# A two-layer decoder step: the indexer-key pages fetched by SyncE, one plain DMA a page, in place of GpSimd's indirect DMAs

## What is computed

```
ki_past = cki[page_table].reshape(B, past, IDX_DIM)
ki_all  = jnp.concatenate([ki_past, ki_new], axis=1)
sc      = indexer_scores(qi, wi, ki_all, q_pos, jnp.arange(L))
_, sel  = lax.top_k(sc, topk)
```

## Time and profile before

| | |
|---|---|
| median of 3 runs | 1708.08 us |
| lowest, highest | 1706.55, 1710.25 us |
| profiled execution, span | 1881.7 us; the page gives no other time of it |
| granted TensorE clock, mean | 0.859 of full speed |
| TensorE busy | 1567.8 us (83%) |
| VectorE, ScalarE, GpSimd busy | 850.0, 482.0, 272.5 us |
| GpSimd page gathers (L626) | 128, 122.0 us busy |
| DMA | 116.45 MB, mean 62 GB/s |

### The profile page before, as it was taken

One profiled execution on the slowest core, in us unless ns is written; L12 is line 12 of the kernel. 1 busy time (PEld: TensorE's weight loads), 2 busy tenths in 40 slices (PEclk: granted clock), 3 DMA queues, 4 the chain that ended last, 5 costly groups with the idle time before them and its releaser, 6 DMA issues.

```text
span 1881.7 us, 29237 instructions
## 1 busy us (share of the span) xinstructions
PE 1567.8 (83%) x10216; PEld 1330.8 (71%) x10216; DVE 850.0 (45%) x1731; ACT 482.0 (26%) x867; POOL 272.5 (14%) x260
## 2 busy tenths in 40 slices
PE   5369967748979999999862999766698999999996
PEld 3146644426969999999830758543487999998996
DVE  1003875624375555642210268753334655557221
ACT  4011301313342222332120132023234322224221
POOL 3710020150020000000176002004102000000002
PEclk8579977657989999999965996957678999999997
DMA  5112101010223333323311211011002233332331
GB/s 163 53 59 59 24 6 53 6 41 1 68 57 90 90 93 95 92 77 93 97 46 44 82 24 23 6 54 32 15 23 68 68 90 92 94 92 73 93 96 46
DMA packets 189622, 116.45 MB, mean 62 GB/s; under 512 B 25716, under 2 KB 184908, under 8 KB 189306
## 3 DMA queue, kind: packets, MB, share of 16 engines
q1 hardware_dynamic: 183246, 102.50, 19.7%
q0 software_dynamic: 6272, 12.63, 2.4%
HBM read 111.30 MB, written 4.44 MB: 62 GB/s over the span
## 4 chain that ended last, share of the span: by engine, by line
PE 72%; issue 12%; DVE 7%; ACT 3%; another core or an unknown queue 2%; DMA 1%; POOL 1%; DVEq 1%; SPq 0%; ACTq 0%; POOLq 0%
PE ps L740 44%; PE ps L725 6%; PE ps L765 4%; PE ps L837 3%; PE ps L984 2%; PE ps L1005 2%; PE ps L828 2%; PE ps L993 1%; POOL xT L620 1%; PE ps L854 1%; PE ps L712 1%; PE ps L788 1%; PE ps L1031 1%; DVE TS L1451 1%
## 5 line engine op out<-in xcount | busy, mean ns | idle before, releaser
L740 PE MATMUL ps<-moR_r,W_r 128*128 128x260 f32 x1408 | 284.8, 284 | 0.0
L740 PEld LDWEIGHTS ps<-moR_r,W_r 128*128 128x128 f32 x1408 | 219.0, 190 | 0.0
L620 POOL TENSOR_TENSOR xT<-xT,moR 128x520 f32<-128x520 f32 x32 | 45.6, 1462 | 1031.9 <-DVE moR L1468 1031.9
L740 PE MATMUL ps<-hT_r,QZC_r 128*128 128x260 f32 x896 | 183.9, 287 | 0.0
L725 PE MATMUL ps<-hT,W 128*128 128x260 f32 x576 | 163.4, 431 | 0.0
L765 PE MATMUL ps<-W,hT 128*128 128x328 f32 (+1 forms) x160 | 81.2, 609 | 94.5 <-issue 91.6
L740 PE MATMUL ps<-moR_r,QZC_r 128*128 128x260 f32 x704 | 148.5, 293 | 12.1 <-DVE hT_r L1810 11.8
L740 PE MATMUL ps<-moR_r,SQ_r 128*128 128x260 f32 x704 | 143.7, 285 | 0.0
L740 PEld LDWEIGHTS ps<-hT_r,QZC_r 128*128 128x128 f32 x896 | 142.4, 194 | 0.0
L740 PE MATMUL ps<-hT_r,SQ_r 128*128 128x260 f32 x704 | 141.4, 282 | 0.0
L765 PEld LDWEIGHTS ps<-W,hT 128*128 128x128 f32 (+1 forms) x160 | 33.4, 223 | 139.3 <-issue 129.4
(11 more groups left out here) (328 smaller groups left out, 3063.0 us busy)
## 6 DMA issues: line engine op xcount, KB each, us to landing
W<-in_w_gate SPq DMA_DIRECT2D x44, 512.0 KB, 3.9
W<-in_w_val SPq DMA_DIRECT2D x44, 512.0 KB, 3.9
W<-in_w_down SPq DMA_DIRECT2D x16, 1408.0 KB, 7.0
W<-in_w_in SPq DMA_DIRECT2D x8, 1024.0 KB, 5.6
W<-in_w_in SPq DMA_DIRECT2D x16, 256.0 KB, 4.2
W<-in_w_out SPq DMA_DIRECT2D x16, 256.0 KB, 4.1
W<-in_w_out SPq DMA_DIRECT2D x8, 512.0 KB, 5.1
yR<-in_x_prompt SPq DMA_DIRECT2D x1, 2048.0 KB
```

What stands on the lines that cost most here:

```text
L620: nc.gpsimd.tensor_tensor(xT[:, k, :], xT[:, k, :], mo[:, k, :], ALU.add).then_inc(x_ready.sem, 1)
L740: last = mm(ps[:, 2 * (g % 2) + f, 0:HT], w(k), x(k)[:, f * HT:(f + 1) * HT], start=(k == 0 and n == 0), stop=(k == nk - 1 and n == 2))
```

## The change

SyncE now fetches the pages. For each of the 128 pages of a layer it loads the page number from the table `PT` in SBUF into a register (`value_load`), computes the address, and issues one DMA of 64 rows of 512 bytes into 64 partitions; even pages go to the lower 64 partitions, odd ones to the upper. The first 64 pages stand behind `load(1)`, the other 64 behind `load(2)`. SyncE waits for the page table at the start of the program (`const_in`), and for `x_turned` ahead of the pages. `idxI`, its constant `row64` and the step on it are gone; GpSimd issues no DMA for pages. The words on constants that only go away are left out of the diff:

```diff
--- before
+++ after
...
@@ -288,7 +287,6 @@
         att = sb("att", [P, 4, 4])
 
         PT = sb("PT", [P, NB, NPG], I32)
-        idxI = sb("idxI", [P, NB, NPP], I32)
         phys = sb("phys", [P, 2, NB, NPP])
         base = sb("base", [P, 1])
         qib = sb("qib", [P, NB, 16])
...
@@ -323,7 +321,7 @@
         w_in_slot = [Signal("w_in_slot0", 16 * SLOT_DMAS[0]), Signal("w_in_slot1", 16 * SLOT_DMAS[1])]
         w_val_slot = [Signal(f"w_val_slot{u}", 16 * NF // 2) for u in range(2)]
         vec_in = Signal("vec_in", 16 * 9)
-        pages_in = Signal("pages_in", 16 * 64)
+        pages_in = Signal("pages_in", 16 * NB * NPG)
         prep_mm = Signal("prep_mm", 1)
         prep_ev = Signal("prep_ev", 4)
         x_ready = Signal("x_ready", 16)
...
@@ -466,6 +463,7 @@
                          A["page_table"].rearrange("b j -> (b j)").partition_broadcast(P)).then_inc(const_in.sem, 16)
             sp.dma_start(x_rows, A["x_prompt"][0].rearrange("(t p) d -> p t d", p=P)).then_inc(x_in.sem, 16)
             sp.dma_start(xs_rows, A["x_sample"][:, 0, :]).then_inc(x_in.sem, 16)
+            sp.wait_ge(const_in.sem, 32)
 
             def layer(l):
                 w_in = A["w_in"][l].rearrange("(k p) n -> p k n", p=P)
...
@@ -502,6 +500,17 @@
                                      ).then_inc(s, 16)
 
 
+                def index_pages(batches):
+                    cache = A["cache_idx_k"][l]
+                    sp.wait_ge(x_turned.sem, KD)
+                    for b in batches:
+                        for j in range(NPG):
+                            page = sp.value_load(PT[0:1, b, j:j + 1], min_val=0, max_val=N_PHYS - 1)
+                            pp, g = divmod(j, 2)
+                            sp.dma_start(IK[64 * g:64 * g + 64, NPP * b + pp, :],
+                                         cache[bass.ds(page, 1)].rearrange("n (r e) d -> (n r) (e d)", e=2)
+                                         ).then_inc(pages_in.sem, 16)
+
                 wait_alone(sp, *so_ev(l, 0))
                 v = vec_rows
                 for a, name in enumerate(("g_pre_mix", "g_post_mix", "g_pre_ffn", "g_post_ffn")):
...
@@ -518,8 +527,10 @@
                 wait_alone(sp, *tile_done(l, 0))
                 load(0)
                 load(1)
+                index_pages(range(0, NB // 2))
                 wait_alone(sp, *kv_mm(l, 5))
                 load(2)
+                index_pages(range(NB // 2, NB))
                 for c in (3, 4):
                     wait_alone(sp, *tile_done(l, 2 * (c - 2)))
                     load(c)
...
@@ -601,10 +612,9 @@
 
         @block.gpsimd
         def _(gp):
-            page_pairs = A["cache_idx_k"].rearrange("l n (r e) d -> (l n r) (e d)", e=2)
             k_rows = A["cache_k"].rearrange("l n r h d -> (l n r) (h d)")
             v_rows = A["cache_v"].rearrange("l n r h d -> (l n r) (h d)")
-            gp.wait_ge(tables.sem, 3)
+            gp.wait_ge(tables.sem, 1)
             gp.wait_ge(x_turned.sem, KD)
 
             def cos_part(l, j):
...
@@ -621,14 +631,6 @@
                                             ).then_inc(x_ready.sem, 1)
 
             def layer(l):
-                wait_alone(gp, *tile_done(l, 0))
-                for j in range(64):
-                    nc.gpsimd.indirect_dma_start(
-                        IK[:, j, :], None, page_pairs,
-                        bass.IndirectOffsetOnAxis(ap=idxI[:, j // NPP, j % NPP:j % NPP + 1], axis=0)
-                    ).then_inc(pages_in.sem, 16)
-
-
                 wait_alone(gp, *rstd_ready(l, 1))
                 for j in range(4):
                     wait_alone(gp, *evac(l, XP_T + j + 1))
...
@@ -654,10 +656,6 @@
                 for j in range(4, 8):
                     cos_part(l, j)
 
-                wait_alone(gp, *pages_in(l, 16 * 64))
-                nc.gpsimd.tensor_scalar(idxI[:, :, :], idxI[:, :, :], float(N_PHYS * 64), None, ALU.add
-                                        ).then_inc(pool_step.sem, 1)
-
                 wait_alone(gp, *list_ready(l, 1))
                 gp.dma_start(scratch.rearrange("b (h i) -> h b i", h=16), ixi[:, :, :]).then_inc(list_out.sem, 16)
                 wait_alone(gp, *list_out(l, 16))
...
@@ -670,7 +668,6 @@
                                 dst[:, 2 * b + t, :], None, rows,
                                 bass.IndirectOffsetOnAxis(ap=IDX[:, b, t:t + 1], axis=0)).then_inc(s.sem, 16)
                 add_updates(l, 0)
-                wait_alone(gp, *pool_step(l, 1))
                 add_updates(l, KD)
 
             with gp.Fori(0, DEPTH) as l:
...
@@ -855,7 +852,7 @@
                                   KIS[:, g % 2, i * P:(i + 1) * P], qib[:, q // NPP, :], start=True, stop=True)
                     last.then_inc(sdot_mm.sem, 1)
 
-                pe.wait_ge(*pages_in(l, 16 * 64))
+                pe.wait_ge(*pages_in(l, 16 * NB * NPG))
                 for g in range(16):
                     pe.wait_ge(*(dot_relu(l, 24) if g < 2 else pg_ev(l, g - 1)))
                     for i in range(4):
```

More of the change, by code:

```diff
@@ L53 @@
           ("swap", P), ("mask", 896), ("same", 64), ("below", 64), ("newneg", 1), ("newrow", 64),
-          ("newto", 64), ("diag", 8), ("iota16", 16), ("tok", 1), ("row64", 1), ("edge", 60), ("wsel", 32),
+          ("newto", 64), ("diag", 8), ("iota16", 16), ("tok", 1), ("edge", 60), ("wsel", 32),
           ("bits", 32)]
@@ L106, in constants @@
     put("tok", np.arange(P)[:, None])
-    put("row64", np.arange(P)[:, None] % 64)
     put("edge", np.array([[w / min(t + 1, w) for t in range(POOL_BUF)] for w in WINDOWS]).reshape(1, 60))
@@ L428, in build @@
         ffn_step = Steps("ffn_step", 5)
-        pool_step = Signal("pool_step", 1)
         SQUARES_ROOM = (4, 4, KD, 2)
@@ L1435, in _ @@
             dve.wait_ge(const_in.sem, 32)
[L1436 to L1439, removed]
             nc.vector.tensor_copy(phys[:, :, :, :], PT[:, :, :].rearrange("p b (j two) -> p two b j", two=2)
```

## The result

| | median, us | runs from to, us |
|---|---|---|
| before, on the same chip | 1709.16 | 1706.55 to 1718.23 |
| after | 1910.7 | 1902.9 to 1912.31 |

After / before is 1.1152, 95% interval 1.1113 to 1.119: slower by 201.5 us. The forecast was slower, 1876 us between 1760 and 2015: the sign and the mechanism came, the size was 35 us short. The profiled execution of the changed kernel took 1911.08 us, its span is 1909.2 us: this time the profile and the timed runs agree, where before they were 174 us apart.

The account below looks back on a forecast made before the run. TensorE's order of work was taken to count, its stalls beside gathers mostly the profile's. Weights queued behind SyncE's page steps came late: 80.2 + 81.0 + 7 for restarts = 168 us on 1708, 1876 us, range 1760 to 2015.

Parts of the forecast that it names:

- the two places named: TensorE waits some 17 us for chunk 2 after two indexer-query tiles, some 60 us for chunk 3 before the first pooling tile.
- Removed gathers: On GpSimd, 128 gathers of 0.951 us leave; nobody waits for them in time, so worth 0.
- the stalls: TensorE's stalls beside gathers, together 160 us, belong mostly to the profiled execution; the 105 us beside page gathers cannot be won.
- B: Rival: the stalls beside the gathers are real in timed runs too, and go; 63 us slower, 1771 us; chance 0.08.
- C: Rival: the stalls are real and the page step is below 1.0 us; 1656 us at 0.80; chance 0.05.
- A: Rival: the register load is about free (0.04), step 0.7 us; 14 us a layer, about 1740 us; chance 0.05.
- D: Rival: the step costs more than 1.8 us, up to 2.45; 307 us more, 2183 us; chance 0.06.
- The step: On SyncE, one page's issue: 0.48 ordinary issue, 0.17 extra register instructions, 0.60 register load; 1.25 us.
- The restarts: TensorE starts at a low granted clock after idling: 2 us a restart, 7 us in all.
- part 2: SyncE's price for the pages: 1.25 us a step, 80 us for 64 steps, 160 us for 128.
- Part 3: Weight chunks queue behind SyncE's page steps: chunk 3 late for the first pooling tile by 80.2 and 81.0 us.
- The stalls at the key and value gathers: In TensorE's profile, excess of 23.8 us in layer 0, 31.0 in layer 1; to stay, span about 1944 us.

Follow-up runs that it names:

- run 3: The changed kernel without the range check on each page number (two check instructions a step): 1834.62 us, ratio 1.073 to the kernel before.
- 4: The changed kernel with the same 128 DMAs but constant page numbers, so no register load and no check: 1739.27 us, ratio 1.017 to the kernel before.
- run 7: The changed kernel with one register load for four page numbers and no check, steps placed as in the change: 1781.67 us, ratio 1.0405 to the kernel before.
- 8: The changed kernel with grouped register loads, no check, steps divided 44, 32 and 52 behind chunks 1, 2 and 4: 1701.7 us, ratio 0.9949 to the kernel before.
- run 2: The kernel before without its page gathers, GpSimd filling the page buffer with a constant instead: 1713.08 us, ratio 1.0029.
- run 10: The kernel before plus one line of the change, SyncE waiting for the page table before its first small loads: 1707.48 us, ratio 1.0005.
- run 1: The kernel before, unedited, measured and profiled anew: 1710.38 us, ratio 1.002, profiled span 1697.4 us.
- 9: The changed kernel with grouped loads, no check and divided steps, measured a second time beside the kernel before: 1700.56 us, ratio 0.9952.
- run 11: The changed kernel with a layer's 128 page steps replaced by two plain 2 MB DMAs behind chunk 1: 1704.32 us, ratio 0.9964 to the kernel before.

## Why the prediction was right, and where it was short

**Right: what decides.** The chunks stand behind 64 and 128 steps, and TensorE waits for them at the two places named, ended by a DMA into `W`; runs 3, 4 and 7 scale as the step does, and 8 takes the delay away by place and price together. Removed gathers are worth 0 (run 2), the wait for the page table 0 (run 10).

**Right: the stalls.** They were not to be won (runs 1 and 2), so B and C fall on their common condition. C needed a step below 1.0 us as well; run 7 has one, 0.85 us, and is slower by 72.5 us. The prediction's A and D fall by the step, 1.34 us.

**The step: 1.34 us measured, 1.25 predicted, by errors that cancel.** SyncE's groups on the lines of a page step in the changed kernel, as min/median/max ns:

```profile
L508 SPq TENSOR_LOAD <-PT x256: 262/268/484, 24.4 to 1124.1; - x128
L508 SPq FUSED_REGOPS  x256: 161/164/179, 24.9 to 1124.4; - x128
L508 SPq SEQ_ASSERT  x256: 18/18/37, 25.1 to 1124.6; - x128
...
L510 SPq FUSED_REGOPS  x256: 113/113/127, 25.2 to 1124.7; - x128
L510 SPq MOVE yR<-in_cache_idx_k x256: 29/29/38, 25.4 to 1124.9; - x128
L510 SPq DMA_DIRECT2D yR<-in_cache_idx_k x256: 468/469/600, 25.5 to 1124.9; - x128
```

The register load, put at 0.60, is 0.268 us (0.33 less): the geometric middle of the two bounds, 0.27, which the prediction worked out and passed over, was the better choice; 0.60 was the middle of two guesses and rests on no row. The DMA was taken from a row of another shape at 0.296 and is 0.469 (0.17 more). Three register instructions at 0.037 became four of 0.164, 0.018, 0.113 and 0.029, together 0.324 for 0.111 (0.21 more): one that checks a range or computes an address from a register is not the one that a fixed address has. The gaps are 0.28 (0.04 more). In all 0.09 us over. That 1.25 came so near is luck: with 0.27 for the load and the rest as it stood, the step would have been 0.92 and the forecast 1876 - 256 x 0.33 = 1792 us.

On the load, the Trainium skill's "DMA: Bandwidth & Descriptors", section "Latency and other measured facts", has a floor of about 600 ns for a `tensor_load`. The row above and that of run 3 have medians of 268 and 267 ns over 256 loads each, so here the measurement decides:

```profile
L508 SPq TENSOR_LOAD <-PT x256: 260/267/488, 24.8 to 1049.4; - x128
```

**The 35 us.** TensorE waited 33.23 + 65.66 = 98.9 us in layer 0 and 96.2 in layer 1, where the prediction had a lateness of 80.2 and 81.0: 34 us more. The restarts, put at 7 us in all, took 2.8 + 2.3 us in layer 0 and 2.5 + 2.2 in layer 1 (tiles of 9.98, 9.48, 9.68 and 9.34 us for 7.18): 9.8. Of layer 0's 18.7 us, 15.8 lie in the first wait: it was to be 109.6 - 92.2 = 17.4 us and was 33.2. Two sources of about equal size are behind the error in layer 0:

- Chunk 3 was to be there at 190.1 and its tile began at 202.58, 12.5 us later: 128 x 0.09 = 11, and the steps began at 24.4 and not at 24.0. That is the step of part 2.
- The tile was wanted earlier. Part 3 had it "for the first pooling tile at 157.58 - 47.7 = 109.9"; without any stall (run 1) it is at 97.27, 12.6 us sooner. The stall was taken out at 0.398 us a record, the pace of the 16 records before it; undisturbed, 48 of them take 13.60 us, 0.283 each, so 40 x (0.398 - 0.283) = 4.6 us were left in. The other 8.0 lie ahead of the stretch: its last 40 records (41, counted by TensorE's own) began at 57.5 in the first profile and at about 60.8 - 40 x 0.283 = 49.5 in run 1. Only the part from 57.5 on had been looked at as disturbed.

These are 25 us, and the waits of layer 0 are only 18.7 over. In the changed kernel's execution TensorE was 2.3 us later at the 48 records than in run 1 (49.62 for 47.28), and the first restart's 2.8 us stand in another term; 1 us is left. In layer 1 the waits are 15 us over; 11 of them are the step again.

**Wrong: what the profile would show.** The stalls at the key and value gathers were to stay, with a span near 1944. From 418 to 461 us, the stretch where they would be in layer 0 (GpSimd issues its 32 gathers there), TensorE is busy 35.29 of 43 us:

```profile
418.00:461.00 43.00, 35.29 (x167) 21.05 (x166) 22.65 (x51) 19.02 (x47) 30.75 (x32) 0.84 0.19 50
```

The span is 1909.2, 2 us from its own time. None of the later profiled executions shows them. The prediction took them for the profiler's, and they were that one execution's. What slowed that one execution stays open; it did not come back.

**Open: the last 0.5%.** Runs 8, 9 and 11 are 0.36 to 0.51% faster than before, run 2 is not (1.0029). The gathers on GpSimd are gone in all; run 2 has a memset of 6.92 us on GpSimd in their place, and its step on `idxI` is still there. The wait for the page table is ruled out (run 10). One thing goes with it: the granted clock. Its mean over the executions was 0.9079 in 8 and 0.9112 in 9, against 0.9023 and 0.9048 in the kernel before beside them, and 0.9052 against 0.9035 in 11. The 72 executions of the kernel before that the ratios rest on differ among themselves by 9.2 us for 0.01 of granted clock. By that slope, an estimate, 5.1, 5.9 and 1.6 us go with the clock, of gains that are 8.9, 8.0 and 5.2 us by the means; 2 to 4 us are left in each. Whether the higher clock is a cause or itself comes of the change stays open. A kernel as 8 that also gathers into a buffer nobody reads would bear on it; it was not run. The gain is shown, its cause is not.

## What to carry to other kernels

Before moving issues to another queue, multiply the whole step (load, checks, address, DMA, gaps) by its count and lay it over what stands behind it in that queue: 128 gathers on an engine for which nobody waited were free, and 256 plain DMAs, each cheaper to issue (0.469 us for 0.951), in front of the weights cost 200 us. If the steps must stand there, load several register values at once, leave range checks out of the loop where the data is sure, and divide the steps over the slack between the loads, by the timeline. And hold a profile's span against the timed runs before building on one of its stretches; a second profile of the same kernel settles it.

## What was not expected of the hardware

- A register load from SBUF takes 0.268 us for one number and 0.298 for four next to each other, 0.07 a number.
- A plain DMA of 64 rows of 512 bytes takes SyncE 0.469 us to issue, one of 66 such rows of `conv_w` 0.296; the page from a register or a constant makes no difference (0.469, 0.468), and why the two shapes differ is open. Two of 2 MB take 8.48 us together in layer 0 and 13.72 in layer 1 (run 11).
- Range check and address on SyncE are single fused instructions of 0.164 and 0.113 us, 2.5 to 4.4 times that of a fixed address (0.037 to 0.046).
- DMA beside TensorE did not slow it where run 1 shows them together. In the repeat of the kernel before, from 30 to 61 us, the gathers run and the DMA engines move 52 GB/s in all; TensorE is busy 29.02 of 31 us at full granted clock, through the key and value columns at which the first profile had its stalls:

```profile
30.00:61.00 31.00, 29.02 (x103) 16.55 (x104) 6.62 (x12) 14.14 (x27) 23.58 (x25) 1.00 0.18 52
```

The Trainium skill says so in "SBUF — State Buffer", section "SBUF: two separate sides" (ports of engines and DMA are disjoint): this trace agrees, and the rows of the first profile, which seemed to speak against it, are not what the gathers do: in run 1 the same gathers run and the stalls are absent.
